# Experts' gated rows added to the residual in DRAM by accumulating scatters; router weights waited for at the router

## The reference, cut to what matters

```
h2 = rms_norm(x1) * (1.0 + sc2) + sh2
# hier_moe(h2): one group of 4 by argmax, then the top 2 of its 4 experts, weights top_w
hid = silu(h2 @ w_gate[e]) * (h2 @ w_up[e])            # e: 16 experts, 1024 -> 256
out = sum over the two chosen e of (hid * top_w) @ w_down[e]
y   = x1 + g2 * out                                     # g2 differs for prompt and sample
```

## Time and profile before

| what | value |
|---|---|
| median of 3 runs | 1587.72 us |
| time of the profiled execution | 1587.63 us |
| its span, first to last instruction | 1585.9 us |
| PE busy in the span | 1376.0 us (87%) |
| VectorE busy | 770.6 us (49%) |
| ScalarE busy | 458.6 us (29%) |
| GpSimd busy | 178.2 us (11%) |
| bytes moved by DMA | 205.85 MB |
| mean granted clock of TensorE | 0.938 |

### The profile page before, as it was taken

One profiled execution on the slowest core, in us unless ns is written; L12 is line 12 of the kernel. 1 busy time (PEld: TensorE's weight loads), 2 busy tenths in 40 slices (PEclk: granted clock), 3 DMA queues, 4 the chain that ended last, 5 costly groups with the idle time before them and its releaser, 6 DMA issues. The chain is left out here.

```text
span 1585.9 us, 20591 instructions
## 1 busy us (share of the span) xinstructions
PE 1376.0 (87%) x7461; PEld 798.6 (50%) x7462; DVE 770.6 (49%) x1683; ACT 458.6 (29%) x989; POOL 178.2 (11%) x366
## 2 busy tenths in 40 slices
PE   3899997979999899999689998899943999999960
PEld 2555553656644566666456665544423454444430
DVE  0421224868496798889755563423344111111118
ACT  3321112232455466663235551011110111111110
POOL 0000002022010111112100000000001223222220
PEclk9999997989989999999899999999975999999985
DMA  8400016752131442230130003522348468775728
GB/s 323 170 3 4 31 51 156 220 174 31 26 86 38 143 133 74 69 124 29 64 131 1 1 1 142 169 97 86 113 143 298 156 219 276 262 272 196 264 95 321
DMA packets 138826, 205.85 MB, mean 130 GB/s; under 512 B 27205, under 2 KB 102917, under 8 KB 138533
## 3 DMA queue, kind: packets, MB, share of 16 engines
q1 hardware_dynamic: 122524, 160.08, 30.9%
q0 software_dynamic: 10272, 32.49, 5.7%
q10 hardware_dynamic: 5946, 12.15, 2.3%
HBM read 158.71 MB, written 43.98 MB: 128 GB/s over the span
## 5 line engine op out<-in xcount | busy, mean ns | idle before, releaser
L2233 PE MATMUL ps<-ex_wgu,ex_xT 128*128 x416 | 185.1, 598 | 4.0 <-ACT ex_xT L2272 2.5
L1390 DVE TENSOR_SCALAR_CACHE_REDUCE tk_eq<-sc,tk_cand 128x512 bf16<-128x512 f32 (+4 forms) x155 | 146.8, 1007 | 0.0
L2233 PEld LDWEIGHTS ps<-ex_wgu,ex_xT 128*128 128x128 f32 x416 | 77.8, 192 | 93.1 <-issue 93.1
L1788 PE MATMUL ps<-hT,mergedT 128*128 128x512 f32 (+1 forms) x288 | 120.1, 600 | 4.9 <-DMA op_wr<-in_w_route_expert 4.9
L1324 PE MATMUL ps<-zT,gt_w 128*128 128x352 f32 (+1 forms) x384 | 120.9, 468 | 0.0
L1324 PE MATMUL ps<-hT,gt_w 128*128 128x352 f32 (+1 forms) x336 | 105.8, 468 | 0.0
L2306 DVE SCALAR_TENSOR_TENSOR ex_hid<-ex_silu,ex_weight,ps 128x256 f32<-128x256 f32 x26 | 12.5, 480 | 185.0 <-ACT ex_silu L2278 185.0
L1324 PEld LDWEIGHTS ps<-zT,gt_w 128*128 128x128 f32 x384 | 73.0, 190 | 44.1
L2254 PE MATMUL ps<-ex_wd,ex_hidT 128*128 x208 | 93.6, 593 | 0.2 <-DVE ex_hidT L2313 0.2
L1353 ACT ACTIVATE mask<-sc,tk_cand 128x384 bf16<-128x384 f32 (+1 forms) x62 | 82.3, 1329 | 15.0 <-DVE tk_cand L1406 15.0
L1788 PEld LDWEIGHTS ps<-hT,mergedT 128*128 128x128 f32 (+1 forms) x288 | 50.9, 186 | 68.4 <-issue 62.7
(11 more groups left out here) (468 smaller groups left out, 2134.1 us busy)
## 6 DMA issues: line engine op xcount, KB each, us to landing
ex_wgu<-in_w_gate SPq DMA_DIRECT2D x16, 1024.0 KB
ex_wgu<-in_w_up SPq DMA_DIRECT2D x16, 1024.0 KB
ex_wd<-in_w_down SPq DMA_DIRECT2D x16, 1024.0 KB
sp_ada_w<-in_w_ada SPq DMA_DIRECT2D x9, 1024.0 KB
cb_y<-y_dram ACTq DMA_DIRECT2D x16, 512.0 KB, 7.6
merge_left_dram<-qiT SPq DMA_DIRECT2D x8, 544.0 KB, 6.1
mg_gb<-gate_b_dram SPq DMA_DIRECT2D x8, 544.0 KB, 3.8
mergedT<-merge_left_dram SPq DMA_DIRECT2D x8, 544.0 KB, 4.7
```

Source lines behind the costliest of these rows:

```text
L1390: return v.tensor_scalar(junk[j], m.sc[0:r, c:c + w], scalar, 0.0, op, ALU.add, accum_out=cnt[0:r, j:j + 1])
L1788: i = nc.tensor.matmul(m.ps[rows, 2 * (t % 2) + n, :], m.mergedT[:, k, t * P:t * P + r], m.wout[:, k, n * 512:(n + 1) * 512], start=k == 0 ...
L2233: j = nc.tensor.matmul(m.ps[:, 2 + b, :], xT[:, b, k, :], wgu[:, bass.ds(at, 1), k, :].rearrange("p o n -> p (o n)"), start=k == 0, stop=k ...
```

## The change

In output_projection the two waits of PE move from ahead of the first `main` to the first `route`. After the last store SP now copies one row of g1 values to all 128 new spare rows at the end of `x1_dram` (so that they hold finite numbers), waits for that, and then loads g2. Routing gives the scatter the row of `x1_dram` itself, the same for both choices, and one spare row per partition for unused slots; it adds three VectorE instructions: a table that says which slots belong to sample rows (`of_sample`, two instructions) and the difference of the two g2 rows. In experts the loads of x1 are gone; VectorE builds the gate rows of a tile from that table (`gate_rows`, into the memory of `hT`), and one VectorE multiplication of 1024 columns replaces the two half copies. The scatter adds to `x1_dram` (`compute_op=ALU.add`) and waits for the one before it, since both may add to the same row. combine is replaced by nine DMAs from DRAM to DRAM, four on SP's queue and five on ScalarE's.

```diff
@@ output_projection
+                sp.dma_start(m.x1_dram[NT:, :], m.modA[:, 0, 0, :]).then_inc(x1d, 16)
+                sp.wait_ge(x1d, 16)
                 load_mod_rows(m, sp, m.gate2, (5,), g2l)
...
                 def route(t):
                     r = rows_of(t)
+                    if t == 0:
+                        pe.wait_ge(wl, 32)
+                        pe.wait_ge(one, 4)
...
-                pe.wait_ge(wl, 32)
-                pe.wait_ge(one, 4)
                 for t in range(TILES + 3):
@@ routing
+                step(v.memset(m.of_sample[:, :], 0.0))
+                step(ts(m.of_sample[:, 0:MAXT], m.by_slot[:, 0, 0:MAXT], float(SEQ), None, ALU.is_ge))
+                step(tt(m.gate2[:, 0, 1, :], m.gate2[:, 0, 1, :], m.gate2[:, 0, 0, :], ALU.subtract))
@@ experts, SP
-                for t in range(TILES):
-                    sp.dma_start(m.x1[t][0:rows_of(t), :], m.x1_dram[t * P:t * P + rows_of(t), :]).then_inc(m.x1l, 16)
@@ experts, POOL
                 def weights(i, b):
...
+                    nc.gpsimd.tensor_copy(scol[:, b:b + 1], m.of_sample[:, bass.ds(n, 1)]).then_inc(wc, 1)
                 def scatter(i, b):
...
-                    wait_alone(3 + 2 * b, yea, n + 1)
                     wait_alone(4 + 2 * b, yed, n + 1)
+                    if b or not (isinstance(i, int) and i == 0):
+                        wait_alone(9 + b, ys[1 - b], 16 * i + 16 * b)
                     nc.gpsimd.indirect_dma_start(
-                        out=m.y_dram, out_offset=bass.IndirectOffsetOnAxis(ap=row[:, b:b + 1], axis=0),
-                        in_=yo[:, b, :], in_offset=None).then_inc(ys[b], 16)
+                        out=m.x1_dram, out_offset=bass.IndirectOffsetOnAxis(ap=row[:, b:b + 1], axis=0),
+                        in_=yo[:, b, :], in_offset=None, compute_op=ALU.add).then_inc(ys[b], 16)
@@ experts, VectorE
                 def rows(i, b):
                     wait(dve, ys[b], 16 * i)
                     dve.wait_ge(dn, 2 * i + b + 1)
-                    v.tensor_copy(yo[:, b, 512:D], m.ps[:, 5, :]).then_inc(yed, 1)
+                    dve.wait_ge(gr, 2 * i + b + 1)
+                    v.tensor_tensor(yo[:, b, :].rearrange("p (c n) -> p c n", c=2), m.ps[:, 4:6, :],
+                                    gate[:, b, :].rearrange("p (c n) -> p c n", c=2), ALU.mult).then_inc(yed, 1)
+                def gate_rows(i, b):
+                    n = 2 * i + b
+                    wait(dve, yed, n - 1)
+                    v.scalar_tensor_tensor(gate[:, b, :], m.gate2[:, 0, 1, :], scol[:, b:b + 1], m.gate2[:, 0, 0, :],
+                                           ALU.mult, ALU.add).then_inc(gr, 1)
                 def body(i):
                     for b in range(2):
                         hidden(i, b)
-                        previous(rows, i, b)
+                        gate_rows(i, b)
                         hidden_copy(i, b)
                         xts(i + 1, b)
+                        previous(rows, i, b)
@@ ScalarE's half copy (rows, L2283) is removed; combine is replaced by
+def results(nc, m, O):
...
+            for t in range(0, PT, 2):
+                sp.dma_start(O.y_prompt[0, t * P:(t + 1) * P, :], m.x1_dram[t * P:(t + 1) * P, :]).then_inc(stored[0], 16)
...
+            for t in range(1, PT, 2):
+                nc.scalar.dma_start(O.y_prompt[0, t * P:(t + 1) * P, :], m.x1_dram[t * P:(t + 1) * P, :]).then_inc(stored[1], 16)
+            nc.scalar.dma_start(O.y_sample[0, :, :], m.x1_dram[SEQ:NT, :]).then_inc(stored[1], 16)
```

More of the change, by code:

```diff
@@ L2104, in experts @@
         yo = sb("ex_y", [P, 2, D])
-        idle = sb("ex_idle", [1, 9])
+        scol = sb("ex_of_sample", [P, 2])
+        gate = flat(m.hT)[:, 0:2 * D].rearrange("p (b n) -> p b n", b=2)
+        gr = m.sem("ex_gate_ready")
+        idle = sb("ex_idle", [1, 11])
         gl, ys = ([m.sem(f"ex_{n}{i}") for i in range(2)] for n in ("x_gathered", "y_stored"))
-        ic, wc, rc, tp, xed, xea, gp, slr, hr, htp, htc, dn, yea, yed, here = (m.sem("ex_" + n) for n in (
+        ic, wc, rc, tp, xed, xea, gp, slr, hr, htp, htc, dn, yed, here = (m.sem("ex_" + n) for n in (
             "index_copied", "weight_copied", "row_copied", "x_transposed", "xT_by_dve", "xT_by_act", "gate_up_psum", "silu_ready",
-            "hid_ready", "hid_transposed", "hidT_ready", "down_psum", "y_by_act", "y_by_dve", "weights_here"))
+            "hid_ready", "hid_transposed", "hidT_ready", "down_psum", "y_by_dve", "weights_here"))
         idle_set = m.sem("ex_idle_set")
@@ L2278, in silu @@
                     nc.scalar.activation(sl[:, b, :], m.ps[:, 2 + b, 0:FD], ACT.Silu).then_inc(slr, 1)
[L2280 to L2283, removed]
                 def body(i):
@@ L2287, in body @@
                         silu(i, b)
-                        previous(rows, i, b)
                         xts(i + 1, b)
-                run(act, body, lambda: (xts(0, 0), xts(0, 1)), lambda last: rows(last, 1))
+                run(act, body, lambda: (xts(0, 0), xts(0, 1)))
             @block.vector
@@ L2322, in body @@
                         hidden(i, b)
-                        previous(rows, i, b)
+                        gate_rows(i, b)
                         hidden_copy(i, b)
                         xts(i + 1, b)
+                        previous(rows, i, b)
                 run(dve, body, lambda: (xts(0, 0), xts(0, 1)), lambda last: rows(last, 1))
[L2330 to L2358, removed]
-                        nc.scalar.dma_start(y[0:r, b, c, :], m.y_dram[c * NT + t * P:c * NT + t * P + r, :]).then_inc(yl[b], 16)
-            @block.sync
-            def _(sp):
-                for t in range(TILES):
-                    sp.wait_ge(orr, t + 1)
-                    dst = O.y_prompt[0, t * P:(t + 1) * P, :] if t < PT else O.y_sample[0, :, :]
-                    sp.dma_start(dst, y[0:rows_of(t), t % NB, 0, :]).then_inc(os_[t % NB], 16)
-                for i in range(NB):
-                    sp.wait_ge(os_[i], 16 * ((TILES - i + NB - 1) // NB))
@@ new lines, in results, with _ @@
+def results(nc, m, O):
+    stored = [m.sem(f"y_stored{i}") for i in range(2)]
+    with nc.Block() as block:
+        @block.sync
+        def _(sp):
+            for t in range(0, PT, 2):
+                sp.dma_start(O.y_prompt[0, t * P:(t + 1) * P, :], m.x1_dram[t * P:(t + 1) * P, :]).then_inc(stored[0], 16)
+            sp.wait_ge(stored[0], 64)
+        @block.scalar
+        def _(act):
+            for t in range(1, PT, 2):
+                nc.scalar.dma_start(O.y_prompt[0, t * P:(t + 1) * P, :], m.x1_dram[t * P:(t + 1) * P, :]).then_inc(stored[1], 16)
+            nc.scalar.dma_start(O.y_sample[0, :, :], m.x1_dram[SEQ:NT, :]).then_inc(stored[1], 16)
+            act.wait_ge(stored[1], 80)
```

18 lines of the change are left out of this document (8 added, 10 removed).

## The result

The changed kernel takes 1596.84 us (median of 8 runs, 1592.36 to 1602.68), the kernel before 1587.12 (8 runs): a ratio of 1.0068, 95% interval 1.0048 to 1.0087. It is slower by 0.7%, where 1576 was forecast; the rival with this sign, "slow add", had 0.22. The profiled execution took 1592.36 us with a span of 1590.5, which is 4.6 more than before. It was the fastest of the eight; the medians differ by 9.7 us, so about 5 us of the loss lie outside what this trace shows. This is how the 4.6 us divide by the terms of the prediction.

The account below looks back on a forecast made before the run. The loop was taken as PE's while inputs come in time, the last stage as mostly transfer. Terms -4.7 + 2.7 + 1.6 - 4.6 + 8 + 3.3 - 18.0 = -11.7 took 1587.63 to 1576 us, range 1562 to 1612.

Parts of the forecast that it names:

- slow add: Rival, chance 0.22: an accumulating scatter occupies the engines four times as long as a plain one, D = 5.1; 1622 us.
- Term 1: Start of output_projection: PE no longer waits there for the router's weights, -4.7 us (bounds -3.1 and -4.7).
- Term 2: End of output_projection: the spare rows' store ahead of the g2 load costs +2.7 us (bounds +1.7 and +3.4).
- Term 3: Routing: three more VectorE steps in a chain that everything waits for, +1.6 us.
- Term 4: Start of experts: first gathers come sooner without SP's nine x1 loads, -4.6 us (bounds -1 and -5).
- Term 5: Experts loop: scatters and gathers go out later, gathers have 6.4 us instead of 8.46; +8 us, from the tight tiles.
- the tight tiles: Experts loop: six tiles where experts have one tile each and gathers come late; at most 13 us more, at least 0.
- D: Time a scatter occupies the 16 engines: plain 1.28 us, accumulating taken as 2.56; PE stalls in every tile from 3.5.
- Term 6: End of experts: the last scatters go out and land later, +3.3 us (bounds +0.7 and +8.3).
- Term 7: Last stage: DRAM-to-DRAM copies, a copied byte costing a load plus a store; 24.8 us instead of 42.8, -18.0.
- fast copy: Rival, chance 0.13: the last stage's DRAM-to-DRAM data takes 10.6 us, all else as forecast; 1565 us.
- gains eaten: Rival, chance 0.19: D near 3.8 and the tight tiles at their bound of 13 us give 1590, no change.

Follow-up runs that it names:

- run 10: The kernel before with only the router's wait moved from PE's first main to its first route: 1583.17 us, ratio 0.9969.
- run 1: The changed kernel with VectorE's order of before (output rows ahead of the copies of hidT and xT): 1573.51 us, ratio 0.9914.
- run 2: The changed kernel with a plain scatter instead of an accumulating one (the sum is left out): 1569.19 us, ratio 0.988.
- run 7: The changed kernel with VectorE's order of before (output rows first) and plain scatters: 1565.31 us, ratio 0.9853.
- run 8: The changed kernel with output rows first on VectorE and a dummy POOL fill between the scatter and the next gather: 1579.23 us, ratio 0.9949.
- run 9: The changed kernel with output rows first on VectorE and a dummy POOL fill right ahead of the accumulating scatter: 1598.02 us, ratio 1.0065.

## Why the prediction was wrong

**Terms 1 to 4** were right: each came within 0.8 us (the table), and run 10 shows the first alone. Term 2 was nearest to a miss, at 3.5 just beyond its bound of 3.4: the g2 load went out 4.1 us behind the store's issue, where 2.6 to 3.4 and a step had been taken.

**Term 5 failed**, and with it the sign. The prediction's order of events was right: output ready 1.9 us later (measured 2.47 us behind the transposes against 0.74, so 1.7), gather behind scatter in one queue. (Its "2.3 us of new work" on VectorE is 1.8 by its own rows, as the half copy of 0.69 goes; it was hidden either way.) Two steps failed. The first is the room: "the scatter goes out that much later, and the gather queued behind it 2.0 us later ... So it has 6.4 us". The gather went out 2.6 to 2.9 us later and had 5.6 to 5.9. Left out were POOL's longer issue of an accumulating scatter (1.60 against 1.01 us), of which the trace of before shows nothing and for which no bound was set, and the added wait for the other scatter (0.45 us of issue instead of 0.16 in every second tile). The estimate of the landing, 5.6 us, was met on the median; but "still under 6.4" compared two fixed numbers with 0.8 us between them, where landings spread over 1.5 us. With that room, the forecast's own 5.6 us is already at the edge; and the room ends some 1.6 us ahead of the transposes, as the stalled tiles show, so that for the odd tiles it was 4.1 us.

The second is the price of being late, taken as the excess alone in ordinary tiles ("from there each us costs 24 us"). A wait of 0.3 us costs a further 1.2 us behind it, as rows of before had shown for the tight tiles; the prediction charged that there and not here. Behind four of the eleven stalls the clock fell as well: after waits of 3.12, 3.46 and 3.57 us, and after one of 0.43 us with 1.26 behind it, the gate_up took 7.8 to 9.1 us instead of 7.13 (granted clock 0.73 to 0.83 over these four stretches). The eleven stalls add up to 11.8 us of waits for gathers and 10.7 us ahead of the gate_ups behind them; PE's records are 10.7 us longer. Stalls in every tile were to begin at D = 3.5; D came out at 3.3, between its lower bound and slow add's 5.1 and beside 2.56 taken, and every second tile stalls already. Runs 1, 2, 7, 8 and 9 show the dependence in their loops: with the scatter 2 us behind the transposes 306 (plain) and 315 to 316 us (add), with 3 us 312 and 331 to 333.

The Trainium skill ("DMA: Bandwidth & Descriptors", SDMA does more than copy) has the add inline with the data stream, and gives no price; that D would stay 1.28 by it was the prediction's inference. The trace speaks against the inference: 3.3 us of engine time, and 6.0 us to land.

**Term 6** had the right steps; the last scatter landed 6.0 us after issue instead of the 4.7 taken.

**Term 7** had the right mechanism and took the wrong one of two bounds: the copy stands near "a copied byte costs as much as one loaded or stored", since 16.8 us is near its 14.2 and far from 24.8. With the engines full the copies ran at 341 GB/s (the window from 1575), loads and stores at 421, so a copied byte cost 1.2 times a loaded or stored one and not twice. That "fast copy" rival held as to the stage; its 1565 fell with term 5.

The same page of the Trainium skill (Latency and other measured facts) gives 207 to 214 GB/s for copies of tiles whose 16 KiB rows lie 512 KiB or more apart, and less at other distances; the prediction left the distance out. The copies here are contiguous blocks of 512 KB, another case: 4.46 MB took 16.8 us with the start of the stage and its wait included, which is 265 GB/s.

**Rivals.** The time is between "gains eaten" and "slow add", with a loss in the loop of 31 us (slow add has 41, on top of the 8 for the tight tiles that its 1622 still contains) at a D of 3.3, where it needed some 4.2 to turn 0.5% slower, and a gain in the last stage that none of the rivals combined with a loss in the loop. That the forecast isn't further off is luck: in the profiled execution term 5 missed by 23 us, and term 7 covered 8 of them from the other side.

## What to carry over

When a DMA is queued behind another on the same engine, work out its room from the issue of the first to the need for the second, with every instruction between (the longer issue of a new kind of DMA as well). Read the need off a tile that already stalls; it can lie ahead of the first instruction that reads the data, here by 1.6 us. Compare the room with the spread of landings, not with a median. A change that moves a producer later and makes the transfer ahead of the next input longer takes from the same room twice, so price the two together. Where the input doesn't depend on the output, issue its load first: here that alone turned 0.7% lost into 1.6% won.

## What the runs showed of the hardware beyond that

- An accumulating indirect scatter of 128 rows of 4 KB held POOL 1.60 us (a plain one 1.01), and the records of the three small copies issued behind it overlap its own and show 0.72 to 0.76 us each, where behind a plain one they show 0.2. Landing with no other traffic: 6.0 us against 3.4.
- A gather issued behind such a scatter lands 8.1 to 8.3 us after the scatter's issue on average, whether it is issued 2.46 us or 3.66 us behind it (runs 1 and 8).
- From tile 6 on, a gate_up in the loop never started sooner than 1.9 us (even tiles) or 2.4 us (odd tiles, behind which the loop's next pass begins) after the landing of the gather whose transposes stand ahead of it, in any of the thirteen traces, whether the clock was at 1.00 or near 0.50 and whether or not the transposes themselves waited. It doesn't read that gather's data: it works on the tile before. Between the two stand waits and two reads of table entries into registers; what fills the time isn't shown, and the releaser that the profile's page names can't be it.
